# Weights of a fused three-layer transformer kernel moved from ten equal slots into two longer rings with build-time places

## The reference

```python
for layer in range(2):
    y = rms_norm(h, nw[0])
    y = even_mixer(y, ...) if layer % 2 == 0 else odd_mixer(y, ...)
    h = h + rms_norm(y, nw[1])
    y = conv_ffn(rms_norm(h, nw[2]), w_up, conv_w, conv_b, w_down)
    h = h + rms_norm(y, nw[3])
# second block
proj = rms_norm(x, g_mix) @ w_in                 # 3 attentions, a forget gate, 3 branch gates
merged = sigmoid(a_m) * (y_m @ w_br_moba) + sigmoid(a_f) * (y_f @ w_br_fox) + sigmoid(a_c) * (y_c @ w_br_mem)
x = x + merged @ w_out
x = x + (silu(h2 @ w_gate) * (h2 @ w_up)) @ w_down
```

## Time and profile before

| what | value |
|---|---|
| median of 3 runs | 1095.84 us (1094.64 to 1097.82) |
| profiled execution, its own time | 1095.88 us |
| its span, first to last instruction | 1094.1 us |
| PE busy | 1086.6 us, 99% of the span |
| PEld busy | 959.6 us, 88% |
| DVE busy | 748.6 us, 68% |
| ACT busy | 600.4 us, 55% |
| DMA moved | 192.29 MB, mean 176 GB/s |

### The profile page before, as it was taken

One profiled execution on the slowest core, in us unless ns is written; L12 is line 12 of the kernel. 1 busy time (PEld: TensorE's weight loads), 2 busy tenths in 40 slices (PEclk: granted clock), 3 DMA queues, 4 the chain that ended last, 5 costly groups with the idle time before them and its releaser, 6 DMA issues.

```text
span 1094.1 us, 16723 instructions
## 1 busy us (share of the span) xinstructions
PE 1086.6 (99%) x6712; PEld 959.6 (88%) x6712; DVE 748.6 (68%) x1109; ACT 600.4 (55%) x994; POOL 109.1 (10%) x127
## 2 busy tenths in 40 slices
PE   8999999999999999999999999999999999999998
PEld 7988989888888899898888888889999989888887
DVE  7876595998846566859788566766656885666651
ACT  6744465776734545557667445357444644555640
POOL 4020000121100000001111001121000000111100
PEclk9999999999999999999999999999999999999999
DMA  8751356666664755366566656474433555666661
GB/s 287 284 174 59 121 206 211 193 190 188 185 192 152 269 150 146 126 225 189 187 190 184 195 182 212 135 234 135 115 99 113 167 159 196 189 181 187 192 193 39
DMA packets 56957, 192.29 MB, mean 176 GB/s; under 512 B 6832, under 2 KB 9776, under 8 KB 56880
## 3 DMA queue, kind: packets, MB, share of 16 engines
q1 hardware_dynamic: 56880, 191.22, 55.2%
HBM read 190.15 MB, written 1.05 MB: 175 GB/s over the span
## 4 chain that ended last, share of the span: by engine, by line
PE 95%; DVE 2%; POOL 1%; ACT 1%; issue 0%; DMA 0%; DVEq 0%; ACTq 0%; POOLq 0%
PE ps L929 28%; PE ps L1019 19%; PE ps L1010 15%; PE ps L1020 10%; PE ps L1285 5%; PE ps L1159 3%; PE ps L1105 3%; PE ps L1082 2%; PE ps L1346 2%; PE ps L1094 1%; PE ps L1031 1%; PE ps L1144 1%; DVE lo L1485 1%; POOL hr L533 1%; PE ps L1051 1%; PE ps L1169 1%
## 5 line engine op out<-in xcount | busy, mean ns | idle before, releaser
L1485 DVE TENSOR_TENSOR lo<-raw,hi 128x1024 fp32r<-128x1024 f32 (+2 forms) x347 | 429.1, 1263 | 81.9 <-ACT hi L588 79.1
L588 ACT ACTIVATE hi<-raw 128x1024 fp32r<-128x1024 f32 (+2 forms) x347 | 347.0, 1036 | 82.2 <-DMA raw<-in_weights 75.5
L1019 PE MATMUL ps<-y_both,hi 128*128 128x512 f32 x912 | 320.8, 397 | 0.0
L1020 PE MATMUL ps<-y_both,lo 128*128 128x256 f32 x912 | 255.0, 280 | 0.0
L1019 PEld LDWEIGHTS ps<-y_both,hi 128*128 128x128 f32 x912 | 171.3, 188 | 41.5
L1020 PEld LDWEIGHTS ps<-y_both,lo 128*128 128x128 f32 x912 | 171.9, 189 | 0.0
L1010 PE MATMUL ps<-y_both,hi 128*128 128x256 f32 x912 | 167.6, 285 | 0.3 <-DVE lo L1485 0.3
L1010 PEld LDWEIGHTS ps<-y_both,hi 128*128 128x128 f32 x912 | 141.8, 191 | 1.1 <-DVE lo L1485 0.5
L1010 PE MATMUL ps<-y_both,lo 128*128 128x256 f32 x456 | 128.9, 283 | 0.0
L929 PE MATMUL ps<-hi,y_both 128*128 128x512 f32 x352 | 94.1, 382 | 2.2 <-DVE lo L1485 1.4
L929 PE MATMUL ps<-hi,h_hi 128*128 128x512 f32 x294 | 90.9, 391 | 0.0
(11 more groups left out here) (291 smaller groups left out, 1386.2 us busy)
## 6 DMA issues: line engine op xcount, KB each, us to landing
raw<-in_weights SPq DMA_DIRECT2D x331, 512.0 KB, 3.7
gain<-in_gains SPq DMA_DIRECT2D x10, 512.0 KB, 7.2
raw<-in_weights SPq DMA_DIRECT2D x8, 384.0 KB, 7.2
bias<-in_rel SPq DMA_DIRECT2D x16, 128.0 KB, 2.1
raw<-in_weights SPq DMA_DIRECT2D x8, 256.0 KB, 2.6
mem_x<-in_mem SPq DMA_DIRECT2D x2, 512.0 KB, 9.8
h<-in_x SPq DMA_DIRECT2D x2, 256.0 KB, 2.7
h<-in_x SPq DMA_DIRECT2D x1, 512.0 KB, 6.1
```

Source lines behind the costliest of these rows:

```text
L588: act.activation(hi[:, s, :w], raw[:, s, :w], ACT.Copy).then_inc(hi_done, 1)
L1019: pe.matmul(dst, hi[:, s, at], y_both[:, :, k, :], start=k == 0, stop=False)
L1020: mm = pe.matmul(dst[:, 0:S], lo[:, s, at], y_hi[:, k, :], start=False, stop=k == KD - 1)
L1485: dve.tensor_tensor(lo[:, s, :w], raw[:, s, :w], hi[:, s, :w].bitcast(F32), ALU.subtract).then_inc(lo_done, 1)
```

## The change

`SLOT` goes. `ring()` now computes, when the program is built, for every unit a place in the hi ring (10480 columns) and one in the lo/raw ring (10384 columns), instead of 10240. `DIST` gives each unit a pair of distances in steps of 16 columns (64 bytes): (tokens to hi, tokens to lo), modulo 128 columns; stages that it does not list keep (0, 0). A unit starts at the next column that has the wanted rest modulo 128; when it doesn't fit before the ring's end it starts at that rest from the ring's beginning. `GIVER[n]` is the last unit that touched any column of either place. The kept part for m_hi and m_lo is now the last 2048 columns of each ring, marked as owned by unit 31 (n - 1 at n = 32). The semaphore that tells of a landing goes by n % 10. To make room, block_causal lies on mk_t, the sinks in unused columns of top and tot, warm is 8 columns and align is gone.

```diff
 LEAD, TAIL, LEADS = 6, 7, 3
+DIST = {"up0": [(7, 4)] * 20 + [(5, 4)] * 18, "up1": [(5, 0)] * 20 + [(3, 4)] * 18, "up2": [(1, 4)] * 20 + [(7, 0)] * 18,
+        "even_f": [(6, 5)] * 4, "even_q": [(5, 2)] * 4, "odd_qk": [(5, 1)] * 8 + [(3, 1)] * 8,
+        "gates": [(1, 7)] * 8 + [(7, 1)] * 8 + [(3, 7)] * 8, "branches": [(7, 3)] * 4 + [(1, 7)] * 4 + [(7, 1)] * 4,
+        "lead0": [(3, 3)] * 6, "lead1": [(5, 5)] * 6, "lead2": [(7, 7)] * 6,
+        "fill": [(1, 7)] * 4 + [(3, 3)] * 4 + [(7, 7)] * 4}
+STEP, LINE = 16, 128
+LO_RING, HI_RING = RAW * UNIT + LINE + STEP, RAW * UNIT + LINE + 7 * STEP
+
+
 def ring():
-    free = [(s, -1) for s in range(FEW)]
+    kept = (RAW - FEW) * UNIT
+    dist = [d for name, n, _, _ in STREAM for d in DIST.get(name, [(0, 0)] * n)]
+    owner = [[-1] * HI_RING, [-1] * LO_RING]
+    end, at, giver = [0, 0], [], []
     for n in range(UNITS):
-        free.append((free[n][0], n))
-        if n == last("fill") - 1:
-            free += [(s, n) for s in range(FEW, RAW)]
-    slot, giver = [x[0] for x in free[:UNITS]], [x[1] for x in free[:UNITS]]
-    return slot, giver, [slot[:n + 1].count(slot[n]) for n in range(UNITS)]
-
-
-SLOT, GIVER, TURN = ring()
+        both, last_owner = [], -1
+        for i, size in enumerate((HI_RING, LO_RING)):
+            if n < last("fill"):
+                size -= kept
+            elif n == last("fill"):
+                owner[i][size - kept:] = [n - 1] * kept
+            rest = STEP * ((7, 0)[i] - dist[n][i]) % LINE
+            p = end[i] + (rest - end[i]) % LINE
+            if p + UNIT > size:
+                p = rest
+            end[i] = p + UNIT
+            last_owner = max(last_owner, *owner[i][p:p + UNIT])
+            owner[i][p:p + UNIT] = [n] * UNIT
+            both.append(p)
+        at.append(both)
+        giver.append(last_owner)
+    return at, giver
+
+
+AT, GIVER = ring()
 TAILS = ["even_out", "down0", "odd_out", "down1", "merge_out", "down2"]
...
-            lo = sb("lo", [RAW, UNIT], F32R, r)
-        raw = sb("raw", [RAW, UNIT])
-        hi = sb("hi", [RAW, UNIT], F32R)
+            lo = sb("lo", [LO_RING], F32R, r)
+        raw = sb("raw", [LO_RING])
+        hi = sb("hi", [HI_RING], F32R)
...
-        m_hi = lo[:, FEW:RAW, :].rearrange("p a (b s) -> p (a b) s", s=S)
-        m_lo = hi[:, FEW:RAW, :].rearrange("p a (b s) -> p (a b) s", s=S)
+        m_hi = lo[:, LO_RING - (RAW - FEW) * UNIT:].rearrange("p (k s) -> p k s", s=S)
+        m_lo = hi[:, HI_RING - (RAW - FEW) * UNIT:].rearrange("p (k s) -> p k s", s=S)
+        def hi_at(n):
+            return hi[:, AT[n][0]:AT[n][0] + UNIT]
+        def lo_at(n):
+            return lo[:, AT[n][1]:AT[n][1] + UNIT]
+        def raw_at(n):
+            return raw[:, AT[n][1]:AT[n][1] + UNIT]
...
-                    sp.wait_ge(unit_used, GIVER[n] + 1)
+                    if GIVER[n] >= 0:
+                        sp.wait_ge(unit_used, GIVER[n] + 1)
-                sp.dma_start(raw[:, SLOT[n], :WIDTH[n]], dram["weights"][n][:, :WIDTH[n]]).then_inc(raw_in[SLOT[n]], 16)
+                sp.dma_start(raw_at(n)[:, :WIDTH[n]], dram["weights"][n][:, :WIDTH[n]]).then_inc(raw_in[n % RAW], 16)
...
-                s, w = SLOT[n], WIDTH[n]
-                act.wait_ge(raw_in[s], 16 * TURN[n])
-                act.activation(hi[:, s, :w], raw[:, s, :w], ACT.Copy).then_inc(hi_done, 1)
+                w = WIDTH[n]
+                act.wait_ge(raw_in[n % RAW], 16 * (n // RAW + 1))
+                act.activation(hi_at(n)[:, :w], raw_at(n)[:, :w], ACT.Copy).then_inc(hi_done, 1)
...
-                s, w = SLOT[n], WIDTH[n]
+                w = WIDTH[n]
-                dve.tensor_tensor(lo[:, s, :w], raw[:, s, :w], hi[:, s, :w].bitcast(F32), ALU.subtract).then_inc(lo_done, 1)
+                dve.tensor_tensor(lo_at(n)[:, :w], raw_at(n)[:, :w], hi_at(n)[:, :w].bitcast(F32), ALU.subtract).then_inc(lo_done, 1)
...
-                s = SLOT[n]
-                    pe.matmul(dst, hi[:, s, at], y_both[:, :, k, :], start=k == 0, stop=False)
-                    mm = pe.matmul(dst[:, 0:S], lo[:, s, at], y_hi[:, k, :], start=False, stop=k == KD - 1)
+                    pe.matmul(dst, hi_at(n)[:, at], y_both[:, :, k, :], start=k == 0, stop=False)
+                    mm = pe.matmul(dst[:, 0:S], lo_at(n)[:, at], y_hi[:, k, :], start=False, stop=k == KD - 1)
```

More of the change, by code:

```diff
@@ L227, in build @@
         mv = sb("mv", [NT, 512])
+        block_causal = mk_t[:, 0, 0:P].bitcast(U32)
         sc = sb("sc", [2, 512])
@@ L243, in build @@
         half = sb("half", [16])
-        warm = sb("warm", [16])
+        warm = sb("warm", [8])
         ss = sb("ss", [2, 2, 2])
@@ L254, in build @@
         rec = sb("rec", [20, 2])
-        snk = sb("snk", [8, 2])
-        esnk = sb("esnk", [8, 2])
+        snk, esnk = top[:, 8:16, :], tot[:, 8:16, :]
         ncum = sb("ncum", [S])
@@ L471, in _ @@
                 (keep[:, :], dram["c_keep"]),
[L472 removed]
+                (window[:, :], dram["c_window"]), (block_causal, dram["c_block"]),
                 (hw[:, :], dram["hgrn_w"].partition_broadcast(P)),
@@ L778, in _ @@
                     act.activation(whole(hg), whole(hg), ACT.Silu).then_inc(hg_evac, 1)
-                    act.activation(warm[:, 8:16], half[:, 8:16], ACT.Exp)
+                    act.activation(warm[:, :], half[:, 8:16], ACT.Exp)
                 if hh in (4, 6):
@@ L785, in _ @@
             act.wait_ge(dve_sink, 1)
-            act.activation(esnk[:, :, :], snk[:, :, :], ACT.Exp).then_inc(act_sink, 1)
+            act.activation(esnk, snk, ACT.Exp).then_inc(act_sink, 1)
             even_hi(1, 1, 2)
@@ L888, in _ @@
             gate_copy(11)
-            act.activation(warm[:, 8:16], half[:, 8:16], ACT.Sigmoid)
+            act.activation(warm[:, :], half[:, 8:16], ACT.Sigmoid)
             for b in range(4):
@@ L936, in last_unit @@
                 for c in range(2):
-                    for x, w in ((y[0], hi), (y[0], lo), (y[1], hi)):
-                        mm = pe.matmul(ps[:, 6 + c, :], x[:, k, P:S], w[:, SLOT[n], 512 * c:512 * c + 512],
+                    for x, w in ((y[0], hi_at), (y[0], lo_at), (y[1], hi_at)):
+                        mm = pe.matmul(ps[:, 6 + c, :], x[:, k, P:S], w(n)[:, 512 * c:512 * c + 512],
                                        start=False, stop=x is y[1])
@@ L996, in tokens_by, with features_of @@
                     by_tile(n, TAIL, False, True)
-            def features_of(n, s, outs, y, nk=KD, cols=P, stage=None):
+            def features_of(n, outs, y, nk=KD, cols=P, stage=None):
                 pe.wait_ge(lo_done, n + 1)
@@ L1008, in features_of @@
                         at = slice(k * cols + f * P, k * cols + (f + 1) * P)
-                        for w, x, first, final in ((hi, yh, True, False), (hi, yl, False, False), (lo, yh, False, True)):
-                            mm = pe.matmul(dst, w[:, s, at], x(k), start=first and k == 0, stop=final and k == nk - 1)
+                        for w, x, first, final in ((hi_at, yh, True, False), (hi_at, yl, False, False), (lo_at, yh, False, True)):
+                            mm = pe.matmul(dst, w(n)[:, at], x(k), start=first and k == 0, stop=final and k == nk - 1)
                 return mm
             def features_pair(n, dst):
-                s = SLOT[n]
                 pe.wait_ge(lo_done, n + 1)
@@ L1142, in _ @@
                         k = 2 * (n - FIRST["even_i"]) + kk
-                        for x, w in ((y_hi, hi), (y_hi, lo), (y_lo, hi)):
-                            mm = pe.matmul(ps[:, 4 + t, :], x[:, k, t * P:(t + 1) * P], w[:, SLOT[n], 512 * kk:512 * kk + 512],
-                                           start=k == 0 and x is y_hi and w is hi, stop=k == KD - 1 and x is y_lo)
+                        for x, w in ((y_hi, hi_at), (y_hi, lo_at), (y_lo, hi_at)):
+                            mm = pe.matmul(ps[:, 4 + t, :], x[:, k, t * P:(t + 1) * P], w(n)[:, 512 * kk:512 * kk + 512],
+                                           start=k == 0 and x is y_hi and w is hi_at, stop=k == KD - 1 and x is y_lo)
                 mm.then_inc(unit_used, 1)
@@ L1157, in fill @@
                         wait_unit(n)
-                    for x, w in ((yh, hi), (yh, lo), (yl, hi)):
-                        mm = pe.matmul(ps[:, 6, t * 256:t * 256 + 256], x[:, k, t * P:(t + 1) * P], w[:, SLOT[n], c],
-                                       start=k == 0 and x is yh and w is hi, stop=k == KD - 1 and x is yl)
+                    for x, w in ((yh, hi_at), (yh, lo_at), (yl, hi_at)):
+                        mm = pe.matmul(ps[:, 6, t * 256:t * 256 + 256], x[:, k, t * P:(t + 1) * P], w(n)[:, c],
+                                       start=k == 0 and x is yh and w is hi_at, stop=k == KD - 1 and x is yl)
                     if t == 1 and k % 4 == 3:
@@ L1189, in even_part @@
                     wait_unit(n)
-                for x, w in ((y_hi, hi), (y_hi, lo), (y_lo, hi)):
```

(11 more changed lines are left out.)

28 lines of the change are left out of this document (13 added, 15 removed).

## The result

The changed kernel takes 1110.36 us (median of 4 runs, 1108.57 to 1111.25) against 1096.83 us for the kernel before (4 runs): ratio 1.0121, 95% interval 1.0103 to 1.014. The profiled execution took 1111.17 us with a span of 1109.4 us, 15.3 us more than the span before. The forecast was 1101.7 us: the sign of the likeliest case was right and the time lies in the range, but the loss is more than twice what was forecast.

What follows compares the result with a forecast made beforehand. TensorE was taken to bound the kernel, busy 1086.6 of 1094.1 us. The profiled 1095.9 us, less 20 for the distances, plus 25.8 for stalls and the clock behind them, gave 1101.7 us, range 1074 to 1124.

Steps and rivals of the forecast that it cites:

- the likeliest case: Whole kernel: part of the excess matmul time won, full stalls, 1101.7 us, own range 1086 to 1112, chance 0.42.
- The three places: Fill to even_out and two in odd_out: loads without cover stall TensorE, 7.4 + 1.25 + 5.9 + 7.2 = 21.8 us.
- The other later loads: Loads elsewhere that wait for a later unit: covered by the queue of eight other loaded units, cost 0.
- for most units GIVER is n - 9: Whole ring: it holds fewer units, so most loads wait for unit n - 9 and no longer n - 10.
- The clock after a stall: Behind the stalls: a further loss, bringing the loss in all to 25.8 us (17 to 33) from 21.8 of stalls.
- (A): Fill to even_out: loads of units 32 and 33 wait for the last fill matmul, stall 7.4 us, then another 1.25.
- (B): odd_out: unit 139's load waits for unit 130 and delays `out_hi(1, 0)`, stall 5.9 us.
- (C): odd_out: unit 140's load waits for unit 131 and delays tile 0's norm and L1031's transposes, stall 7.2 us.
- The gain of the distances: Pairs and 256-column matmuls: other distances between tokens and weights make them start closer together, 20 us less.
- the distances do nothing: Rival, whole kernel: no gain from the distances, only the 25.8 us of loss, 1121.7 us, chance 0.22.
- nearly all: Rival, whole kernel: nearly all of the excess matmul time is won, chance 0.24.
- Some distances are worse than 0: Rival, in the pairs: 10 ns more on half of them, nothing elsewhere, 1126 us and above, chance 0.06.

Runs made afterwards that it cites:

- no_stall: Changed kernel with the ring restarting at its beginning at unit 32 and lead0 and lead1 at distance (0, 0), removing the late loads: 1084.71 us, ratio 0.9893.
- giver_139: Kernel before with one change, the load of unit 139 waits for unit 130 instead of 129: 1103.96 us, ratio 1.0072.
- giver_140: Kernel before with one change, the load of unit 140 waits for unit 131 instead of 130: 1105.71 us, ratio 1.0078.
- giver_rest: Kernel before with the changed kernel's later load waits, except units 32, 33, 41, 139 and 140, which keep their old giver: 1096.78 us, ratio 1.0007.
- the maps: Two runs: no_stall with another pair of distances in each unit, the second with the list backwards in each stage: 1148.40 and 1130.09 us.
- best71: no_stall with (5, 0) and (3, 4) in all up stages and (7, 1) in the weight-stationary stages moving 256 token columns: 1078.72 us, ratio 0.9827.
- best33: As best71 with (3, 3) in place of (7, 1): 1082.24 us, ratio 0.9858.
- giver_all: Kernel before, old ten slots and distance 0, with the changed kernel's later load waits, units 32, 33, 41, 139, 140 included: 1125.96 us, ratio 1.0268.

## Why the forecast was off

Its steps in order, against the profiled 1111.17 us:

- *The three places.* Forecast 7.4 + 1.25, 5.9 and 7.2 us = 21.8. In the changed kernel, set against no_stall matmul by matmul, the waits are 7.5 + 1.0, 5.6 and 7.0 = 21.1. Right in place, kind and size, and giver_139 and giver_140 show the last two one by one. The other later loads were costed at nothing, and giver_rest shows that, though "for most units GIVER is n - 9" doesn't hold: it is n - 9 for 152 of the 347 units and n - 10 for 158.
- *The clock after a stall.* Taken as 4 us (25.8 - 21.8) in the forecast's loss, the author's estimate, which no run shows: half of 7.9 us, three times the 2.6 us that a stretch of 5.3 us at half speed loses, as the first warming matmuls begin 0.43 us apart and the later ones 0.216. Measured by the same comparison: 2.6 behind (A), 2.3 behind (B), 1.7 behind (C) = 6.6, with the granted clock at 0.50 behind each. So each of the three stalls throws TensorE back to half speed. Mis-sized by 2.6 us: I took half, and the three waits of 5.6 to 7.5 us brought 6.6 of the 7.9.
- *The gain of the distances.* The 20 us in the forecast's sum are the author's estimate, and no run shows them: this is the step that failed, and with 6.6 us it is most of the 9.5 us between forecast and measurement. Measured 13.4 us: 4.0 in up1, 4.0 in up2, 3.3 in the features stages between down1 and lead2, 1.2 in odd_qk, 1.1 in the three leads, 0.6 up to even_out, 0.1 elsewhere, and 0.9 lost in up0. That is 7.1 us in the pairs and 6.2 in the matmuls of 256 columns; even_f, which was to fall below 120 ns, stayed there. The 13.4 us holds against this one trace of before; where an up stage of before stands at its other rate, as up1 does in giver_rest, it is 2 us less or more. The lowest rates seen at any of the 64 pairs of distances are 340 and 113.3 ns, which in all these matmuls would be 304 x 6.9 + 608 x 13.2 + 2160 x 6.7 ns = 24.6 us, an estimate from the traces of before and the maps; 20 us would have been 81% of it. Nor do the 6.3 ns between up0 and up1 measure what a better place would give: 346.9 and 353.2 ns are two rates of one place, and the changed kernel fell on slower rates of its own in up0 (350 ns) and in parts of the 256-column stages (117.8 and 118.9).
- *A term that was missing*: 1.1 us in even_a (below).

21.1 + 6.6 + 1.1 - 13.4 = 15.4 us, and the spans differ by 15.3. From the forecast: 1101.7 - 0.7 + 2.6 + 1.1 + 6.6 = 1111.3 us.

The rival "the distances do nothing" is refuted by no_stall (1084.71 us, ratio 0.9893). The case "nearly all", the side of faster, needed a gain above the loss of 25.8 us: measured were 13.4, and the 24.6 us above is what the lowest rates of the maps would give. "Some distances are worse than 0" turned out in up0, by 3 ns a pair (350.0 against 346.9), with the others better. best71 and best33 have the same instructions at other distances between tokens and weights, and a matmul of 256 columns takes 113.2 and 117.6 ns. Whether it is the reading that collides, no run here shows.

What stays open is why these distances have these rates, and what in the stream keeps it on one of them. It is open, too, whether the distance is what counts: in every run the tokens lie at the same place modulo 128 columns and only the weights move (the memory tokens `m_hi` of fill, one step off, are the exception), so the place of the weights alone would explain the same rows. No run separates the two operands' reads, and none was made to push a running stream from one rate to the other by anything but another distance.

## What to carry to other kernels

When a ring gives out places by position, print for each unit which other unit's last use it now waits for, and look first at the units that another engine must handle ahead of work of its own that TensorE waits for: 166 loads waited a unit or two longer and cost nothing measurable, and five cost 27.7 us. A steady stream whose rate differs between two equal stages has more than one rate at the same layout (346.9 and 353.2 ns a pair here); then a gain can't be read off that difference, and a layout must be tried in the order in which it will run. The trace of one layout doesn't say what another can reach: a kernel that runs all layouts, one per unit, gives the whole map in one trace (here 340.0 to 355.2 ns a pair, in the order in which they ran).

## What the runs showed of the hardware

- Pairs at (0, 0) run at 346.9 or at 353.2 ns for a whole stage of 38 units. up0, up1, up2 stood at 347, 353, 353 in before, at 353, 347, 353 in giver_139, at 347, 347, 353 in giver_rest and at 353 in all three in giver_all. A stage's change of rate is worth 304 x 6.3 ns = 1.9 us. The 13 times of the kernel before beside giver_all reach from 1093.81 to 1099.55 us; those of best71 lie within 1.7 us, and all its up stages stood at 340. That the rates make this spread is likely but not shown, since only one run of each kernel has a trace.
- At the same program position, GpSimd began its first product of `mem_x` at 18.14 to 18.38 us in four of the traces with the old places, and at 17.84 to 17.96 in all eight with the new ones (giver_139, at half speed there, is left out). There it begins 0.16 us ahead of DVE's last pair of `y_lo` products, where in before it began 0.12 us behind, and this is the pair of operations in the changed kernel:

```profile
17.89 2.99 POOL L585 TENSOR_TENSOR xhat<-mem_x,gain 128x512 f32<-128x512 f32 x2 [4.82 <-DMA mem_x<-in_mem]
18.05 3.38 DVE L1725 TENSOR_TENSOR y_both<-pt,y_both 128x512 fp32r<-128x512 f32 x2
```

  DVE takes 3.38 us for the two where it took 2.40 in before, and TensorE starts its next matmul 1.1 us late. The two happen together in these traces; no run moved the one alone. Why GpSimd starts earlier with the new places wasn't tried.
